# Retention and block-sparse attention step: the first sample sequence's scores move into the last projection chunk, rounded weights leave the value slots, and the page slots are given out anew

## What is computed

```
proj = h @ w_in;  q, k, v, g = split(proj, 4)
q = rmsnorm(q) * qn_g;  k = rmsnorm(k) * kn_g        # per head of 128
k_all = concat(k_past (paged), k);  v_all = concat(v_past (paged), v)
# each query: its own block and the best 3 of 4 past blocks by q . mean(k of block)
s = q k^T * scale - slope * distance;  p = softmax(s over chosen blocks);  o = p v
x = x + gate * ((o * silu(g)) @ w_out)
```

## Time and profile before

| what | value |
|---|---|
| median of three runs | 712.32 us (711.63 to 718.92) |
| the profiled execution | 712.81 us |
| its span | 711.0 us |
| busy PE, DVE, ACT, POOL | 627.3, 375.6, 216.2, 196.0 us |
| moved | 191.70 MB, mean 270 GB/s |

### The profile page before, as it was taken

One profiled execution on the slowest core, in us unless ns is written; L12 is line 12 of the kernel. 1 busy time (PEld: TensorE's weight loads), 2 busy tenths in 40 slices (PEclk: granted clock), 3 DMA queues, 4 the chain that ended last, 5 costly groups with the idle time before them and its releaser, 6 DMA issues.

```text
span 711.0 us, 10913 instructions
## 1 busy us (share of the span) xinstructions
PE 627.3 (88%) x4136; PEld 365.9 (51%) x4136; DVE 375.6 (53%) x685; ACT 216.2 (30%) x458; POOL 196.0 (28%) x221
## 2 busy tenths in 40 slices
PE   3569999999999999899989879999899967759985
PEld 1136666664666566534434247767645535434441
DVE  2461557485656657454230542345727489883722
ACT  2325413524341443110000334554134234321010
POOL 0005046222704430320000038999801011110000
PEclk9869999999999999999999999999999999999999
DMA  9995533893697389737894683354699999999970
GB/s 329 359 383 197 186 121 119 306 315 119 245 345 243 113 297 350 260 144 282 321 387 177 180 301 119 118 190 154 229 406 403 380 403 408 407 401 408 371 301 7
DMA packets 82448, 191.70 MB, mean 270 GB/s; under 512 B 4167, under 2 KB 12359, under 8 KB 82268
## 3 DMA queue, kind: packets, MB, share of 16 engines
q1 hardware_dynamic: 80796, 184.84, 70.7%
q0 software_dynamic: 1264, 4.98, 2.0%
q10 hardware_dynamic: 336, 1.18, 0.4%
HBM read 168.57 MB, written 22.41 MB: 269 GB/s over the span
## 4 chain that ended last, share of the span: by engine, by line
PE 70%; DVE 13%; issue 7%; DMA 4%; ACT 3%; SPq 2%; POOL 0%; DVEq 0%; ACTq 0%; POOLq 0%
PE bank L724 15%; PE bank L977 8%; PE bank L732 8%; PE bank L696 8%; PE bank L715 5%; PE bank L920 4%; DVE ring L1667 3%; PE bank L772 3%; PE bank L940 3%; DMA ring<-in_cache_k 2%; PE bank L811 2%; PE bank L857 2%; DMA x_rows<-in_x_sample 2%; DVE weights_low L527 2%; PE bank L762 1%
## 5 line engine op out<-in xcount | busy, mean ns | idle before, releaser
L724 PE MATMUL bank<-weights_high,h_high 128*128 128x512 f32 x288 | 115.7, 402 | 0.0
L527 POOL TENSOR_TENSOR weights_low<-ring,weights_high 128x512 fp32r<-128x512 f32 x80 | 100.4, 1290 | 53.3 <-PE bank L715 53.3
L724 PE MATMUL bank<-weights_high,h_low 128*128 128x512 f32 x288 | 113.3, 393 | 0.0
L1109 ACT ACTIVATE weights_high<-ring 128x1024 fp32r<-128x1024 f32 x72 | 74.0, 1054 | 89.4 <-PE bank L732 89.4
L732 PE MATMUL bank<-weights_low,h_high 128*128 128x512 f32 x288 | 87.2, 401 | 0.9 <-DVE weights_low L527 0.9
L1505 DVE TENSOR_TENSOR partial_low<-bank,partial_high 128x512 fp32r<-128x512 f32 x34 | 23.4, 690 | 114.1 <-ACT partial_high L1071 72.6
L724 PEld LDWEIGHTS bank<-weights_high,h_high 128*128 128x128 f32 x288 | 54.2, 188 | 27.9 <-issue 15.9
L1667 DVE STREAM_TRANSPOSE ring<-ring 128x1024 f32<-128x1024 f32 x48 | 55.3, 1211 | 21.6 <-DMA ring<-in_cache_k 21.6
L772 PE MATMUL bank<-consts,arena 128*128 128x128 f32 x232 | 38.2, 298 | 26.3 <-ACT arena L1129 11.2
L732 PEld LDWEIGHTS bank<-weights_low,h_high 128*128 128x128 f32 x288 | 52.9, 188 | 14.9 <-DVE weights_low L527 3.9
L724 PEld LDWEIGHTS bank<-weights_high,h_low 128*128 128x128 f32 x288 | 54.3, 189 | 11.8
(11 more groups left out here) (215 smaller groups left out, 883.5 us busy)
## 6 DMA issues: line engine op xcount, KB each, us to landing
ring<-in_w_ada SPq DMA_DIRECT2D x12, 2048.0 KB, 12.9
ring<-in_cache_k SPq DMA_DIRECT2D x48, 512.0 KB, 12.2
ring<-in_cache_v SPq DMA_DIRECT2D x40, 512.0 KB, 9.3
ring<-in_w_ret_in SPq DMA_DIRECT2D x8, 2048.0 KB, 8.7
ring<-in_state_ret SPq DMA_DIRECT2D x32, 512.0 KB, 8.0
out_state_sample<-ring SPq DMA_DIRECT2D x32, 512.0 KB, 5.7
ring<-in_w_moba_in SPq DMA_DIRECT2D x8, 2048.0 KB, 12.9
arena<-in_cache_v SPq DMA_DIRECT2D x24, 512.0 KB, 8.7
```

The lines of the kernel that those rows point to most:

```text
L527: tensor_tensor(w_low[:, slot, k, :], ring[:, slot, k * CH:(k + 1) * CH], high[:, k, :].bitcast(F32), ALU.subtract).then_inc(low_ready[LOW ...
L724: pe.matmul(o[i][:, :], xs[p][i][:, k, :], high[:, k, :], start=k == 0 and p == 0, stop=False)
L1109: nc.scalar.activation(w_high[u[0] == "moba"][:, 2 * i:2 * i + 2, :].rearrange("p a b -> p (a b)"), w[:, 2 * i * CH:(2 * i + 2) * CH], ACT ...
```

## The change

- Scores of sequence 0 are made in chunk 5, after its first pair of high-part matmuls (`rows_and_scores`), and no longer after the chunks. DVE turns four of its pages in chunk 3 and four in chunk 4, and runs softmax 0 in chunk 5.
- The sample rows are done first in chunk 3 (`row_order`), so that their q and k are ready earlier, with a semaphore of their own (`sample_qk`). POOL multiplies them by the gains between two pieces of chunk 4's low part, and multiplies the prompt rows of chunk 3 only after it has padded the queries of sequence 0.
- The low part of chunk 5's weights goes from POOL to DVE.
- The rounded weights of layer 1 move from the second slot and G to G and the half of the padded queries `qd` that is now used second. So the wait for row tile 1 of chunk 5 ahead of slot 4 falls away, and POOL clears that half of `qd` after h is joined. The low part of h moves too. Scores and probabilities of the samples now lie in the constants.
- Scores of sequence 1 stand in step 0, between the prompt's head 0 and gate tile (6, 1). Those of sequence 2 stand at the start of step 1, ahead of the two tiles of chunk 7.
- The order of the loads and their slots are new, and mout 0 comes after values(6), in slot 0, instead of ahead of it in slot 4.

```diff
-SCORES_AT = {0: (0,), 1: (1, 2), 2: (3,), 3: (4,), 4: (5,), 5: (6,), 6: (7,), 7: ()}
+SCORES_AT = {0: (), 1: (2,), 2: (3,), 3: (4,), 4: (5,), 5: (6,), 6: (7,), 7: ()}
-K_SLOTS = (2, 2, 4, 2, 0, 4, 2, 0)
-V_SLOTS = (4, 0, 4, 2, 0, 4, 2, 0)
+K_SLOTS = (2, 2, 4, 4, 2, 0, 4, 2)
+V_SLOTS = (4, 2, 0, 4, 2, 0, 4, 2)
...
-    units += keys(0) + [("moba", 6, 0)] + values(0) + keys(1) + [("moba", 7, 0)] + keys(2) + keys(3) + values(1)
-    for s in range(2, NS - 2):
+    units += keys(0) + [("moba", 6, 0)] + keys(1) + values(0) + [("moba", 7, 0)] + keys(2)
+    for s in range(1, NS - 2):
         units += values(s) + keys(s + 2)
-    return units + [("mout", 0, 0)] + values(NS - 2) + values(NS - 1)
+    return units + values(NS - 2) + [("mout", 0, 0)] + values(NS - 1)
...
-            out.append(SLOTS - 2)
+            out.append(0)
...
                     wait_full(sp, ("pT", 1, 1, 1))
-                    wait_full(sp, ("row", "moba", 5, 1))
...
+            def rows_and_scores(k):
+                if k == 0:
+                    sample_scores(0)
+                turn_rows(k)
...
+                if s == 0:
+                    sample_scores(1)
                 for c, n in GATE_AFTER.get(s, ()):
                     g_chunk(c, (n,))
```

More of the change, by code:

```diff
@@ L259, in bank_plan @@
         pair(("row", "moba", c, 0), ("row", "moba", c, 1))
+        if c == 5:
+            use(("QK", 0), 6)
         if c >= 4:
@@ L923, in sample_scores @@
                 sealed(last, ("QK", s))
+            def rows_and_scores(k):
+                if k == 0:
+                    sample_scores(0)
+                turn_rows(k)
+            for c in range(6):
+                project_parts(("moba", c), ("moba", c, 0), {4: turn_rows, 5: rows_and_scores}.get(c))
             def sample_values(s):
@@ L1213, in _ @@
                     high_weights(("moba", c + 1, 0), range(2, 4))
-                for n in range(3):
+                for i, n in enumerate(row_order(c)):
                     label = ("row", "moba", c, n)
-                    done = 3 * c + n
+                    done = 3 * c + i
                     if c < 4:
@@ L1393, in _, with gained @@
                 wait_full(pool, ("hT", 1, n, 1))
-            nc.gpsimd.memset(L1["qd"], 0.0).then_inc(pool_zeroed, 1)
+            nc.gpsimd.memset(L1["qd"][:, 1, :], 0.0).then_inc(pool_zeroed, 1)
             pool.wait_ge(gains_in, 32)
+            def gained(c, n):
+                which = c // 2
+                wait_read(pool, ("row", "moba", c, n))
+                r = row_qk[:, which, n, (c % 2) * CH:(c % 2 + 1) * CH].rearrange("p (h d) -> p h d", h=4)
+                nc.gpsimd.tensor_tensor(r, r, gains[:, which, :].unsqueeze(1).broadcast_to([P, 4, DH]),
+                                        ALU.mult).then_inc(sample_qk if n == 2 else qk_rows, 1)
             low_weights(pool, nc.gpsimd.tensor_tensor, ("moba", 0, 0))
-            for c in range(5):
+            for c in range(3):
                 low_weights(pool, nc.gpsimd.tensor_tensor, ("moba", c + 1, 0))
[L1399 to L1406, removed]
+                for n in row_order(c):
+                    gained(c, n)
+            low_weights(pool, nc.gpsimd.tensor_tensor, ("moba", 4, 0), lambda k: k == 3 and gained(3, 2))
             pool.wait_ge(qb_ready, 1)
@@ L1424, in _ @@
             pool.wait_ge(low_ready["gpsimd"], KT * sum(e == "gpsimd" for e in LOW_BY.values()))
+            pool.wait_ge(sample_qk, 4)
             pad_queries(0)
             pool.wait_ge(qd_ready, 1)
+            for n in range(2):
+                gained(3, n)
+            pool.wait_ge(qk_rows, 8)
             for n in range(2):
@@ L1777, in _ @@
                     prompt_max(HEAD_AHEAD[s])
-                if 0 < s < NS - 1:
+                if 1 < s < NS - 1:
                     output_rows(s - 1)
+                if s == 0:
+                    prompt_max(HEAD_BETWEEN[0])
+                    for pg in range(PAGES):
+                        turn_page(1, pg)
+                        if pg == 3:
+                            prompt_sums(HEAD_BETWEEN[0])
+                    output_rows(0)
+                    sample_softmax(1, None)
+                    for pg in range(PAGES):
+                        turn_page(2, pg)
                 for q in SCORES_AT[s]:
-                    sample_softmax(q, HEAD_AHEAD.get(s) if q == SCORES_AT[s][0] else None)
-                    last = q == SCORES_AT[s][-1]
-                    if last and s in HEAD_BETWEEN:
+                    sample_softmax(q, HEAD_AHEAD.get(s))
+                    if s in HEAD_BETWEEN:
                         prompt_max(HEAD_BETWEEN[s])
@@ L1787, in _ @@
                             turn_page(q + 1, pg)
-                            if pg == 3 and last and s in HEAD_BETWEEN:
+                            if pg == 3 and s in HEAD_BETWEEN:
                                 prompt_sums(HEAD_BETWEEN[s])
```

190 lines of the change are left out of this document (100 added, 90 removed).

## The result

The changed kernel takes 721.52 us (median of 4 runs, 719.78 to 728.38) against 711.98 us for the kernel before (the three runs above and a fourth). The ratio is 1.016, with a 95% interval of 1.012 to 1.020; by the two medians alone it is 1.013. Executions of one kernel spread with their mean granted clock, here 719.78 us at 0.972 and 728.38 us at 0.956. The forecast was 718.5 with a range of 711.5 to 724.5. So the kernel is slower by the wait for mout 0, as forecast, but takes 3 us more than was forecast. The profiled execution took 721.9 us, its span is 720.1.

What follows compares the result with a forecast made beforehand. Two nearly level bounds were taken: the load stream and the PE and DVE chain releasing its slots. Span 711.0 + 0.3 (chain) + 0 (stream) + 4.1 (wait) + 1.8 (clock) = 717.2; 718.5 us against the median, range 711.5 to 724.5.

Steps and rivals of the forecast that it cites:

- the head start: Load stream: keys 1 issued at 497.9 instead of 513.26, filling 6 us at 501; spent by 590.
- within 1%: Outcome with the time between 705.2 and 719.4 us, not told from no change; chance 0.51.
- Part 1: Scores of sequence 0 inside chunk 5: gate tile starts at 515.5 instead of 515.65, a gain of 0.1 us.
- Part 2: Scores of 1 and 2 earlier: maximum of head 2 at 572.6 instead of 571.82; 0.3 us behind taken.
- The third rival: PE and DVE also fall behind, at scores 2, by 3 to 5 us: 722 to 725 us; chance 0.12.
- Part 3: Load stream: 9 us of slot gaps against 6 us gained; term 0, between 1.5 us early and 2 late.
- the first rival: Load stream stays full, mout 0 is in 6 us earlier, PE does not wait: 707.5 us; chance 0.12.
- Part 4: mout 0 behind values 6 lands at 673.5; PE waits 4.1 us (3.4 to 6) ahead of its tiles.
- The clock: Work behind PE's wait for mout 0 runs at the lower clock: 1.8 us more (0 to 1.8).
- Chain: PE and DVE work releasing the slots, from scores to transposes: 0.3 us behind (0.4 ahead to 3 behind).

Runs made afterwards that it cites:

- e1: The changed kernel with mout 0 ahead of values 6 again: 714.89 us, ratio 1.0036 to the kernel before.
- e2: The kernel before with only mout 0 put behind values 6, its slot 4 unchanged: 721.34 us, ratio 1.0140 to the kernel before.
- e4: The changed kernel with scores 2 between the two tiles of chunk 7 and mout 0 ahead of values 6: 713.08 us, ratio 0.9997 to the kernel before.
- e5: The changed kernel with values 7 not issued before mout 0 has landed: 728.48 us, ratio 1.0162 to the kernel before.
- e6: The changed kernel with mout 0 between the two halves of values 6: 713.79 us, ratio 1.0024 to the kernel before.
- e7: The changed kernel with scores 2 between chunk 7's tiles and mout 0 between the halves of values 6: 713.30 us, ratio 1.0008 to the kernel before.
- e3: The changed kernel with scores 2 between chunk 7's tiles and head 1's maximum after four page transposes: 718.82 us, ratio 1.0100 to the kernel before.
- e8: The changed kernel with PE running the values of sequence 6 ahead of the two mout 0 tiles: 714.79 us, ratio 1.0028 to the kernel before.
- e10: e1 with the first half of values 2 loaded ahead of keys 3: 711.54 us, ratio 1.0009 to the kernel before.
- e9: e4 with the first half of values 2 loaded ahead of keys 3: 707.16 us, ratio 0.9950 to the kernel before.

## Why the prediction was right, and where it was short

**What held.** Mechanism and place: the head start is spent by slot releases, nothing is gained by it, and PE stands still for mout 0 and runs the tiles behind it at a lower clock. e1 and e2 show from both sides that this one edit makes the loss. The chances leaned the other way, 0.51 for "within 1%" beside 0.39 for slower, and slower is what came: the sum stood 3 us low, with its result next to the bound.

**Part 1** held to a few tenths. Taking off the 1.3 us, the gate tile was due at 514.2 and came at 514.26; it took 7.11 us (7.0 taken, not 8.8). The join of h took 4.69 us from 508.84, where about 508.7 was due, so the moves in chunks 3 to 5 cost no more than some tenths.

**Part 2** was too small: its own sum, 572.6 against 571.82, was 0.8 behind, 0.3 was taken and 3.2 measured (573.76, where 571.82 less 1.3 is 570.5). The step that failed is the way from the first tile to the scores of 1, put at 7.3 us as before. It was 9.0 (521.2 to 530.19), of which 1.29 are a wait for the second half of values 0: with keys 1 now ahead of them PE got these pages only at 525.86. Scores 2 took 6.23 us, not 5.7. By scores 3 most was made good, because PE waited 1.20 us there instead of 4.07 and they took 3.66 us instead of 5.14. By the end of scores 7 the chain is 1.5 us late against the trace before (2.8 with the 1.3): the scores of 5 and 6 ran for 5.35 and 6.22 us where it was 3.66 and 5.69. The third rival (the chain 3 to 5 us behind) had this place and, at the maximum of head 2, just its size; about half of it reached the tail.

**Part 3** held in its sum. I had 8.2 us of gaps between 550 and 590; 304 instead of 407 GB/s over 40 us is 10.1. They lie where SP waits for a slot: keys 3 issued at 554.36, keys 4 at 579.71. The stream was 2.5 us in arrears at 590, a little outside the bound of 2 late. No cost of it shows, since the chain was as late: DVE waited for no key page until keys 7, and there 5.51 us, against 5.92 before. That is also why the first rival did not come about. e4 comes nearest to what it wanted: keys 4 are issued at 571.75 instead of 579.71, and the profiled execution has its span of 706, but the median is that of the kernel before.

**Part 4** is the mis-sized term: a wait of 4.1 us taken, 6.05 measured, just over the bound of 6. The load was issued at 659.67 rather than 658 (the chain), and the 15.4 us for values 6 and itself lacked a tail of 1.8 us: it landed at 676.9 and not at 673.5. PE asked for it 1.7 us later too, at 671.1. I had put the tail down as "what of the next transfers mixes in" at nothing; e5, where nothing was behind it and the landing took 17.8 us, speaks against that source. The rows of before had the tail already. The last page of keys 7 took 14.8 us from its issue to its landing at 660.2, and mout 0, issued at 658.12 with that page still to land, took 9.4 us for bytes that need 5.2. And the 14.7 us of the second half of w_out were no twin. It was issued 4.5 us after SP was through with the key pages ahead of it (620.65 to 625.11, the page numbers lie between), mout 0 only 2.3 us after values 6 (657.35), so more was still ahead. Both land alike after the last page ahead of them: 5.4 and 5.3 us. The page "DMA: Bandwidth & Descriptors" of the Trainium skill (Queues, rings and completion order) says that an SDMA engine works its ring in order and that completion isn't in order per issuing engine. The traces here agree with the first half, since mout 0 landed 5.2 to 7.7 us behind the last page ahead of it in every run; no run shows a load that overtakes, which the second half allows.

**The clock.** The tiles behind the wait took 2.92 us more, where 1.8 was taken as the most. In the five executions with a wait of 2.69 us or more for mout 0 they took 15.43 to 16.82 us; behind 1.86 and 2.39 us (e6, e7) they took 13.97. On the other side the first sample tile at the end, 3.52 us before, took 1.92, so 1.6 came back. That was luck, as far as the traces show. In e2, e3, e5, e6 and e7 the value products of sequence 7 took 5.30 to 5.33 us instead of 3.64, and in e1, e8 and e10 the sample tile 3.49 to 3.54; only the changed kernel, e4 and e9 had neither.

**The sum.** Chain +1.5 (0.3), wait and its start +6.2 (4.1), clock 2.9 (1.8) and the sample tile -1.6 (0) make 9.0 us; the spans differ by 9.1. The 1.6 us and the 1.3 us ahead of chunk 3 both fell in the favour of this execution: without them its span would be 723.0, 5.8 over the forecast of 717.2.

## What to carry to other kernels

A load that moves behind others in one queue lands later by their bytes at the stream's rate, and in most runs here it came 5.2 to 6.2 us after the last page ahead of it, so estimate that page's landing first (14.8 to 16.5 us after its issue here) and not only the bytes. Set the result against the moment at which the engine asks for the load, and look whether something whose data are in could run first. A head start of the loads was worth nothing here while each next slot was still released by the same chain: trace the slots, not the bytes. An edit that takes a short dip out of the stream can cost more than the dip, if what stood in it was the load with the least time to spare.

## What the hardware showed that I had not expected

A 2 MB transfer landed after 7.9 to 9.9 us when no pages were issued just ahead of it (before, e1, e4, e9, e10; the last key page landed 2.0 to 3.1 us after its issue), 13.0 and 13.7 with 2.1 MB of pages ahead (e6, e7), and 17.2 to 19.3 with 4.2 MB (after, e2, e3, e5, e8). So what is left over the bytes by the rate is not one number: 1.8 us in the changed kernel, 2.4 in e5, 3.9 in e8. Counted from the landing of the last page ahead it is 5.2 to 6.2 us in the seven runs with pages ahead, and 5.4 to 7.7 in the five others. The tail of the last 4 us in e5, with the share falling to 0.38, appears even though one queue issued it all.

The same idle time gave two speeds of what follows. After 2.07 us of waiting, the scores of 5 took 3.66 us in the kernel before, in e2, e6, e8 and e9, and 5.30 to 5.35 in the kernel after and in e1, e5 and e10. What decides between them is open. In e5 PE did its last matmul at 676.4. The granted clock still stood at 1.00 until 680 and was 0.61 and 0.50 in the two stretches after; the tiles then took 16.04 us.
